# Odd layer: high parts of u ahead of two modulation copies, one low part behind the norm, and a shorter reciprocal root

## The reference

```python
def rms_norm(x, gain):
    y = x32 * lax.rsqrt(jnp.mean(x32 * x32, axis=-1, keepdims=True) + EPS)
    return (y * gain).astype(x.dtype)

def modulate(x, gain, shift, scale):
    return rms_norm(x, gain) * (1 + scale) + shift     # shift, scale, gate: silu(c) @ mod_w + mod_b

def odd_mixer(h, w_in, sg_gain, sg_w, sg_b, conv_w, w_out):
    u, v, hx, bg, cg = jnp.split(h @ w_in, [...], axis=-1)
    v = rms_norm(v.reshape(bsz, length // SG_CHUNK, SG_CHUNK, SG_GROUPS, SG_GROUP_WIDTH), sg_gain)
    s = jnp.einsum('gpq,bnqgc->bnpgc', sg_w, v) + sg_b.T[:, :, None]
    y_c = u * s.reshape(bsz, length, SG_WIDTH)
    zc = conv(cg * hx, conv_w)
    return jnp.concatenate([y_c, bg * zc], axis=-1) @ w_out

h_lat = h_lat + g2 * hier_moe(modulate(h_lat, norm2_g[i], sh2, sc2), *moe_args)   # end of layer i
a = modulate(h_lat, norm1_g[i + 1], sh1, sc1)                                     # start of layer i + 1
```

## Time and profile before

| what | value |
|---|---|
| median of three runs | 1733.77 us |
| the profiled execution, its own time | 1732.0 us |
| its span | 1730.2 us |
| TensorE busy | 1606.2 us, 93% of the span |
| VectorE busy | 827.6 us, 48% |
| ScalarE busy | 727.8 us, 42% |
| GpSimd busy | 475.3 us, 27% |
| mean granted clock of TensorE | 0.975 of full |
| chain that ended last, by engine | TensorE 77%, VectorE 14%, ScalarE 4%, DMA 2% |

### The profile page before, as it was taken

How to read it: one execution, slowest core, us unless ns; L and a number is a source line. 1 busy time by engine, 2 the same in 40 slices (tenths; PEclk the granted TensorE clock), 3 DMA queues, 4 the chain that set the end, 5 groups by cost and what they waited for, 6 DMA issues and landing times.

```text
span 1730.2 us, 24182 instructions
## 1 busy us (share of the span) xinstructions
PE 1606.2 (93%) x10054; PEld 1358.0 (78%) x10054; DVE 827.6 (48%) x1523; ACT 727.8 (42%) x1044; POOL 475.3 (27%) x171
## 2 busy tenths in 40 slices
PE   5999979999799799989999888999999998899997
PEld 4856867787798677878888767999888887789996
DVE  2722678743566786445244255522343432645222
ACT  3423367643334675443223335444332223354442
POOL 1200024522000354216100023554541000246543
PEclk9989889999999999999999999999999999999999
DMA  9578279965742698533533215555444332255550
GB/s 388 186 260 296 77 280 343 351 222 195 277 147 112 254 343 330 207 118 117 174 134 144 100 53 198 189 195 181 160 150 158 118 146 98 83 186 196 185 192 25
DMA packets 46621, 327.28 MB, mean 189 GB/s; under 512 B 5424, under 2 KB 5424, under 8 KB 8752
## 3 DMA queue, kind: packets, MB, share of 16 engines
q1 hardware_dynamic: 46512, 325.73, 52.5%
HBM read 324.66 MB, written 1.05 MB: 188 GB/s over the span
## 4 chain that ended last, share of the span: by engine, by line
PE 77%; DVE 14%; ACT 4%; DMA 2%; issue 1%; POOL 1%; DVEq 0%; ACTq 0%; SPq 0%
PE ps L201 25%; PE ps L204 17%; PE ps L206 16%; PE ps L205 16%; DVE lo L212 6%; DMA raw<-in_wmod 2%; ACT hi L209 1%; PE ps L2535 1%; DVE ar L212 1%; DVE gl L212 1%; DVE big L220 1%; POOL lo L212 1%; DVE ar L2586 0%; DVE xn L212 0%; ACT ar L209 0%
## 5 line engine op out<-in xcount | busy, mean ns | idle before, releaser
L212 POOL TENSOR_TENSOR lo<-raw,hi 128x2048 fp32r<-128x2048 f32 (+2 forms) x84 | 393.6, 4695 | 680.0 <-ACT hi L209 680.0
L209 ACT ACTIVATE hi<-raw 128x2048 fp32r<-128x2048 f32 (+2 forms) x216 | 396.2, 1863 | 34.9 <-PE ps L206 19.4
L212 DVE TENSOR_TENSOR lo<-raw,hi 128x2048 fp32r<-128x2048 f32 (+1 forms) x132 | 343.4, 2621 | 111.5 <-ACT hi L209 111.5
L201 PE MATMUL ps<-hT,raw 128*128 128x256 f32 x1024 | 231.4, 382 | 0.0
L201 PEld LDWEIGHTS ps<-hT,raw 128*128 128x128 f32 x1024 | 191.0, 190 | 29.5 <-issue 4.0
L204 PE MATMUL ps<-hTh,hi 128*128 128x256 f32 x640 | 184.5, 288 | 10.7 <-DVE lo L212 6.0
L205 PE MATMUL ps<-hTl,hi 128*128 128x256 f32 x640 | 183.5, 287 | 0.0
L206 PE MATMUL ps<-hTh,lo 128*128 128x256 f32 x640 | 183.5, 287 | 0.0
L204 PE MATMUL ps<-hi,gh 128*128 128x512 f32 x320 | 130.9, 409 | 14.9 <-DVE lo L212 14.8
L204 PEld LDWEIGHTS ps<-hTh,hi 128*128 128x128 f32 x640 | 125.3, 196 | 12.6 <-DVE lo L212 6.5
L204 PE MATMUL ps<-hi,hTh 128*128 128x512 f32 (+3 forms) x320 | 118.7, 371 | 10.9 <-DVE hTl L212 5.4
(11 more groups left out here) (288 smaller groups left out, 2650.6 us busy)
## 6 DMA issues: line engine op xcount, KB each, us to landing
raw<-in_wgu SPq DMA_DIRECT2D x64, 1024.0 KB, 4.8
raw<-in_wmod SPq DMA_DIRECT2D x48, 1024.0 KB, 5.4
raw<-in_wdn SPq DMA_DIRECT2D x32, 1024.0 KB, 4.9
raw<-in_wgt SPq DMA_DIRECT2D x32, 1024.0 KB, 4.9
raw<-in_wup SPq DMA_DIRECT2D x32, 1024.0 KB, 4.8
raw<-in_wdown SPq DMA_DIRECT2D x32, 1024.0 KB, 5.1
raw<-in_wz SPq DMA_DIRECT2D x12, 1024.0 KB, 4.8
raw<-in_wbr SPq DMA_DIRECT2D x8, 1024.0 KB, 6.4
```

The lines of the kernel that those rows point to most:

```text
L201: return self.e.matmul(o, l, r, start=first, stop=last)
L209: return self.e.activation(o, a, f, **kw)
L212: return self.e.tensor_tensor(o, a, b, op)
```

## The change

Three edits in code order:

- `v_rstd` does one Newton step and then one step of third order, 3 + 4 instructions, in place of three Newton steps of 3 instructions. The text of the change calls the results divisors.
- Behind the experts, VectorE's split call before `v_moe_out` has `ahead=0` for `ahead=1`. In layer 0 the low part of the second `ov` chunk is then made at the head of `v_odd`, behind the norm. In layer 1 the same call stands for `z`: the low part of the second z chunk (1248 wide) is then made by the next split call, in `v_z`, behind that norm.
- In `a_odd`, ScalarE makes both high parts of u straight after the sines, before it copies modulation parts 8 and 9.

```diff
@@ v_rstd
-        for _ in range(3):
-            v.wait_ge(*v.last)
-            v.stt(tmp, dst, -0.5, dst, ALU.mult, ALU.mult).then_inc(*v.up("dve"))
-            v.wait_ge(*v.last)
-            v.tt(tmp, tmp, ss, ALU.mult).then_inc(*v.up("dve"))
-            v.wait_ge(*v.last)
-            v.stt(dst, tmp, 1.5, dst, ALU.add, ALU.mult).then_inc(*v.up("dve"))
+        v.wait_ge(*v.last)
+        v.stt(tmp, dst, -0.5, dst, ALU.mult, ALU.mult).then_inc(*v.up("dve"))
+        v.wait_ge(*v.last)
+        v.tt(tmp, tmp, ss, ALU.mult).then_inc(*v.up("dve"))
+        v.wait_ge(*v.last)
+        v.stt(dst, tmp, 1.5, dst, ALU.add, ALU.mult).then_inc(*v.up("dve"))
+        c = 0.375 ** 0.5
+        v.wait_ge(*v.last)
+        v.tt(tmp, dst, dst, ALU.mult).then_inc(*v.up("dve"))
+        v.wait_ge(*v.last)
+        v.stt(tmp, tmp, c, ss, ALU.mult, ALU.mult).then_inc(*v.up("dve"))
+        v.wait_ge(*v.last)
+        v.stt(tmp, tmp, -1.25 / c, tmp, ALU.add, ALU.mult).then_inc(*v.up("dve"))
+        v.wait_ge(*v.last)
+        v.stt(dst, tmp, 1.875, dst, ALU.add, ALU.mult).then_inc(*v.up("dve"))
@@ v_moe
-        self.v_split(v, *(("z", 0, 0, 0) if l else ("ov", 0)), ahead=1)
+        self.v_split(v, *(("z", 0, 0, 0) if l else ("ov", 0)), ahead=0)
         self.v_moe_out(v, l)
@@ a_odd
         self.a_angles(a)
+        self.a_split(a, "u", 0, ahead=1)
         for p in (8, 9):
             self.a_mod(a, 1, p)
@@ v_odd
+        self.v_split(v, "ov", 1, ahead=0)
         for p in (6, 7):
             self.v_mod(v, 1, p)
         self.v_angles(v)
```

## The result

The changed kernel took 1724.92 us (median of 6 runs, 1720.39 to 1730.61) against 1733.99 us (6 runs, 1732.40 to 1735.88) of the kernel before: ratio 0.9936, 95% interval 0.9907 to 0.9965. (This ratio is not the quotient of the two medians; that is 0.9948 and lies inside the interval.) It is faster by more than 0.2%. The profiled execution took 1726.26 us; its span is 1724.4 us, at a mean clock of 0.973. The span is 5.8 us shorter than before, and the difference has three pieces. Ahead of the passage only the roots differ between the kernels, but VectorE's first `ov` low part starts 3.17 us later (426.76 for 423.59). hx starts 5.99 us earlier (471.69 for 477.68), so the passage gained 9.16 us. Behind hx 0.2 us are lost again. The 3.17 us are lost before the passage: the granted clock is low for 3.4 us longer in each of three places there (near 173, 204 and 241 us).

A forecast was written before the change was run, and what follows sets the result against it. TensorE held 77% of the chain, so edits pay only at its stops, mainly 4.15 us before the norm and 4.52 before u. 8.5 + 1.17 = 9.7 us gave 1722.3, or 1724.1 from the median; range 1720.5 to 1729.5.

The forecast's parts named there:

- Rival A: Layer 0's norm matmuls also keep the upper clock level: about 1.1 us more, total 10.8, time 1723.0; chance 0.30.
- Part 1: Layer 0, low part moved behind the norm: third addition 1.31 us sooner, moved low part covered by 0.3 us.
- Part 2: Reciprocal roots, each 0.39 us shorter: five of 13 count, the three outside the passage give 1.17 us; eight are covered.
- Part 3: u's high parts ahead of the copies: the 4.52 us stop at u goes; hx 8.5 us earlier, 1.7 from the norm.
- Part 4: Layer 1, low part moved in z: gains 0; if it slid under GpSimd's pair, costs at most 1.42 us.
- B: u's second load, gating ScalarE, takes 10.5 us: total gain only 4.3 us, time 1729.5; chance 0.10.
- C: Same ScalarE queue, u's second load later still: slower than before, 1738.9 us if it takes 20 us; chance 0.03.
- D: hx, bg or cg loads, or a stop behind hx, take the gain back: time 1732; chance 0.07.

The follow-up runs named there:

- third trace: The changed kernel with no further change, one more run for its trace, beside the kernel before: 1730.77 us.
- second trace: The changed kernel again with no further change, timed against the kernel before: 1724.63 us, ratio 0.9925 (0.9899 to 0.9951).

## Why the prediction was right, step by step

**The result.** Forecast 1724.1 us, range 1720.5 to 1729.5; measured 1724.92. The mechanism was the one forecast. Rival A, on the norm's clock, came true in the first and third trace of the changed kernel and not in the second.

**Part 1** held. Less the 3.17 us by which that trace runs late, the third addition started at 429.86 (forecast 429.91) and the norm's matmuls at 436.30 (436.36). The cover of the moved low part was 0.4 us (0.6 in the second trace), forecast 0.3.

**Part 2** was over-sized in one term. The step that failed: "five lie where VectorE alone holds the chain". At the last norm it is so: from the root's start to the product, 2.26 us for 2.65 (1716.45 to 1718.71, and 1721.89 to 1724.54), 0.39 as said. In both layers with experts it was so only by 0.1 us, behind which the router's matmuls end. From the root's start to TensorE's count, layer 1 took 3.92 us (535.07 to 538.99) for 4.03: 0.11, not 0.39. In layer 0 the root-only version, against the first trace of before, gained 0.12 up to the products of hpl (3.86 for 3.98). In the first trace of the changed kernel layer 0 even lost, since a stretch at the lower clock fell on the router's matmuls: 4.44 us for the 32, and a wait of 0.97 us. So the three roots outside the passage are worth 0.11 + 0.12 + 0.39 = 0.62 us and not 1.17. The row that tells it was in the trace of before and was not read: 32 router matmuls ending at 543.71, the very moment the root was ready. A chain names only what came last, not what came 0.1 us earlier. The two roots in the passage, 0.78 us in part 3, brought 0.3 to 0.5 by the version with the old root. The count was off as well: 15 roots and not 13, so ten are covered and not eight, worth 3.9 us and not 3.1 if every cover were gone. The six in the second model gave nothing, and hid even 1.76 us each; that the four at the start gave nothing fits the traces but is within their spread.

**Part 3** held. u began at 455.60 on before's scale (forecast 456.60 with the norm at the lower clock, and 456.48 in the second trace, which had it). ScalarE began u's first high part at 452.46 less 3.17 = 449.3, forecast 450.5; in the second trace, with the norm's clock as assumed, at 449.96, so 0.7 us of the difference is the clock. The second load gated ScalarE by 0.78 and 0.73 us, where the forecast's own times (452.35 and 452.4) left under 0.1. hx began at 469.14 in the second trace, forecast 469.2. hx's stop was 0.93 and 0.66 us, forecast 0.8. The gain of the passage was forecast as 8.5 us: 54.09 - 45.55 = 8.54 us in the second trace, with the norm's clock as assumed, and 9.16 and 9.34 in the two traces in which it stayed up. Rival A put that at 1.1 us; 0.6 to 0.8 came through. The norm itself was 1.63 us shorter, of which the wait of 0.48 us for GpSimd (445.40) took back a part; u began 0.88 us sooner than in the second trace and hx 0.62.

**Part 4** held: 0. From the last wait ahead of layer 1's scatter (TensorE's row with a wait for hidl, at 752.57 before and 747.86 after) to the wait for GpSimd's low part, 37.28 us before and 37.31 after. The Trainium skill (GPSIMD Engine Reference, Specifications) says that VectorE instructions with two SBUF inputs contend with GpSimd. The trace agrees on both sides: the moved one took 1.45 us with 1.4 us between them, the next one, beside GpSimd, 3.20.

**The sum.** With the term set right it is 8.5 + 0.6 = 9.1 us, or 9.8 where the norm keeps its clock. The medians differ by 9.07 us beside the first runs and by 12.7 beside the second; the first interval reaches from 6 to 16 us, and the second interval, 0.9899 to 0.9951, reaches from 8.5 to 17.5. That the forecast of 9.7 came so near is partly luck: the over-sized root and the under-sized chance of A cancel.

**B, C and D** did not come. u's second load landed 5.3 us after its issue (437.14 + 12.99 - 0.33 = 449.80, to 455.14), and nothing took the gain back between hx and layer 1's root: 63.38 us from one to the other in both kernels (477.68 to 541.06, 471.69 to 535.07).

## What to carry to other kernels

Find what holds a low or high part in its engine's queue, not only the engine that TensorE's stop names: the stop named VectorE, and two copies that waited on TensorE in ScalarE's queue were the cause. Before a shorter chain of small instructions is counted in full, look for the other input of the instruction behind it, and when that one arrived; here it came 0.1 us before. To judge an edit of some us in a run that differs by 10 us from one execution to the next, measure in the trace from a fixed instruction ahead of the edit to one behind it, which repeated to 0.01 us in the kernel before and to 0.2 us in the changed one, and at the same clock.

## What the runs showed of the hardware

- The clock behind a stop of 2.4 us is not fixed by the code. Of six traces with a stop of 2.38 or 2.39 us before the norm, four kept the upper level (32 matmuls in 3.84 us) and two lost it (5.47 and 5.29). Both with 2.78 and 2.79 kept it; the one with 3.77 and all four with 4.15 or 4.16 lost it. Elsewhere in the passage a stop of 2.40 us (`ov`, 25th matmul) kept it, one of 2.73 (hx) lost it, and so did all four of 4.52 (u). The Trainium skill (TensorE: Matmul & The Clock Gate, Why this matters for your kernels) says that short gaps leave the clock up; that holds here in six of the eight stops of 2.38 to 2.79 us before the norm.
- A stop that shrinks can cost as much as before: at 3.77 us the matmuls behind it took 6.26 us, at 4.15 they took 5.47. The lower stretch was 6.8 us long in the first case, from 1.7 us before the norm's first matmul, and 3.4 us in the second, from 0.6 us behind it. Why it lay so differently was not tried.
- Runs of the kernel before lie between 1726.19 and 1748.64 us in the later sets. In thirteen traces VectorE's first `ov` low part, ahead of which only the root differs, starts anywhere from 417.73 to 430.61 us. The stretches at the lower clock in the first 250 us differ as well, 34 to 61 us in all, but their sum does not tell the start: with 34.1 us it was 417.73 in one trace and 423.59 in another. What decides it is open.
